# Gate and up products of a dense SwiGLU layer: high and low input joined into one 512-column matmul, and the bank's halves summed by VectorE

## The chip, the cores and the metric

The kernel runs on one core of one Trainium2 chip. The metric is the device time of one execution in microseconds (us); lower is better.

## What is computed

The reference is a two-layer decoder trunk over 256 tokens of width 1024. Each layer has a token mixer (a gated linear recurrence beside differential attention), a SwiGLU channel mixer, and a per-layer embedding. The channel mixer is dense in layer 0 and picks two of eight experts per token in layer 1. The change touches the dense one:

```python
D_MODEL, SEQ, D_FF = 1024, 256, 3584

def swiglu(h, w_gate, w_up, w_down):
    return (jax.nn.silu(h @ w_gate) * (h @ w_up)) @ w_down

h = rmsnorm(x, norm_g[i, 2])
if i % 2 == 0:
    f = swiglu(h, ffn_w_gate[i // 2], ffn_w_up[i // 2], ffn_w_down[i // 2])
```

## The kernel before

All products are in float32 of reduced precision (fp32r), made more exact by splitting both operands: a high part that TensorE takes as it is, and a low part that holds the rest. A product is the sum of three: high by high, high by low, low by high.

**Chunks.** Weights arrive from memory in chunks of 1 MB, each in one of six `raw` slots of 128 x 2048. ScalarE writes the high part of a chunk into one of three `whi` slots, in two halves (`hi`; in the dense stage L1005); VectorE then writes the low part into `wlo` (`lo`, L1208; in the dense stage L1612). TensorE waits for each half of the low part (`s_lo`), uses the chunk, and reports each half as used (`s_pe`), on which ScalarE waits before it writes the high part of the chunk three further on. SyncE issues the load of a chunk when the low part of the chunk six before it is done (L517).

**The dense stage.** The 3584 hidden channels are cut into 14 pairs of chunks: for pair `s` a gate chunk and an up chunk, each all of the 1024 input channels (8 tiles `k`) by 256 hidden channels (2 tiles `t`). The first two pairs are written out, the other twelve run in a loop of two turns of six. The weights are held in the array and the input moves: `HH` and `HL`, the high and low part of the normalised input, 128 x 8 x 256 each. `chunk8` goes through `k` and `t` and issues the three products of 256 columns by `three` (L1921):

```python
for t in range(2):
    ins = three(B[bank][:, SEQ * t:SEQ * t + SEQ], wslot(b), x,
                (A, slice(256 * k + P * t, 256 * k + P * t + P)), (A, k, A), True,
                k == 0 and t == 0, k == KT - 1)
```

So one PSUM bank of 512 columns holds a chunk's result, 256 tokens for each `t`. Gate chunks use banks 0 and 2 in turn and up chunks 1 and 3. The first chunk of all is `chunk8_first` (L1959, L1961, L1967), which takes the low input last.

**The eviction.** On VectorE `dense` makes, for each of the two chunks, the low part of the chunk three further on and then the chunk's result: `scaled` (L1292) multiplies the bank by `RINV`, the inverse norm of each token, into `FS` (gate) or `FA` (up). ScalarE applies Silu to `FS` (L1008); VectorE multiplies, `FA` = `FS` x `FA` (L1623); ScalarE writes the high part `FH` (L1010), and VectorE the low part `FL` (L1626). The semaphores are `f_g` (gate evicted), `f_u` (up evicted), `f_s` (Silu done), `f_a` (product done), `f_h` and `f_l`. TensorE waits for `f_g` of the pair two before it begins a gate chunk and for `f_a` of that pair before an up chunk.

**The down products.** Fourteen further chunks (`down`) hold the activations and move the weights, 512 columns a matmul (L1910). `three_turned` reads those 512 columns in interleaved halves. They add into banks 4 to 7 (`Z_BANK`).

All four engines run their own instruction lists in the order in which the code issues them; the order of the work is written out by hand.

Of the kernel before, what the change touches and what calls it, by code (L numbers as in the profile page):

```python
# [8 lines left out]
ALU = mybir.AluOpType  # L9
ACT = mybir.ActivationFunctionType  # L10
AX = mybir.AxisListType
F32 = mybir.dt.float32
F32R = mybir.dt.float32r
# [3 lines left out]
P = 128  # L17
# [48 lines left out]
def bass_hybrid_rglru_diffattn_moe(nc, x, p, positions, norm_g, w_in, conv_w, conv_b, lru_wa, lru_ba, lru_wx,  # L66
# [4 lines left out]
    with ctx:  # L71
# [4 lines left out]
        def at(name, off, shape, dt=F32):  # L76
            return nc.alloc_sbuf_tensor_at(name, shape, dt, offset=off)
# [47 lines left out]


        a0 = arena
        HH = at("HH", a0, [P, KT, SEQ], F32R)
        HL = at("HL", a0 + 8 * KB, [P, KT, SEQ], F32R)
        o_rin = a0 + 16 * KB  # L130
        a1 = beside(o_rin, HELD)
        RIN = at("RIN", o_rin, [P, KT, SEQ + 3])
# [119 lines left out]
        def sem(name):  # L252
            return ctx.enter_context(nc.semaphore(name))
# [80 lines left out]
        s_hl = sem("s_hl")  # L334
        f_g = sem("f_g")
        f_u = sem("f_u")
        f_s = sem("f_s")
        f_a = sem("f_a")
        f_h = sem("f_h")
# [99 lines left out]
        block = ctx.enter_context(nc.Block())  # L439

        Z_BANK = ((4, 5), (6, 7))
        M_BANK = ((6, 7), (3, 5))
        PP_BANK = ((0, 4), (1, 5))
        PP_LAST = (5, 0)
# [736 lines left out]
        def _(dve):  # L1181
# [16 lines left out]
            def bank2(n):  # L1198
                return B[n][:, :].rearrange("p (t s) -> p t s", t=2)
# [51 lines left out]
            def inverse_row(i, bank):  # L1251
                dve.wait_ge(s_rt, i)
                link(v.tensor_copy(RINV[:, :], B[bank][:, 0:SEQ]))
# [36 lines left out]
            def scaled(dst, src):  # L1290

                return v.tensor_tensor(dst, src, RINV[:, :].unsqueeze(1).to_broadcast([P, 2, SEQ]), ALU.mult)  # L1292
# [310 lines left out]
            def dense(s, b, it):  # L1603

                q = (b - FFN0) // 2 % 2
                fs, fa = (t[:, q, :].rearrange("p (t s) -> p t s", t=2) for t in (FS, FA))
                for n in range(2):
                    nb = b + n + SPL
                    for e in range(2):
                        dve.wait_ge(s_hi, 2 * nb + e + 1 + 24 * it)  # L1610
                        r = slice(HC * e, HC * e + HC)
                        v.tensor_tensor(wlo[nb % SPL][:, r], raw[nb % RAW][:, r], whi[nb % SPL][:, r].bitcast(F32),  # L1612
                                        ALU.subtract).then_inc(s_lo, 1)
                    if n == 0:
                        if isinstance(s, int) and s == 0:
                            inverse_row(2, 6)
                        scaled(fs, bank2(2 * q)).then_inc(f_g, 1)
                    else:
                        ins = scaled(fa, bank2(2 * q + 1))
                ins.then_inc(f_u, 1)  # L1620
                dve.wait_ge(f_u, s + 1)
                dve.wait_ge(f_s, s + 1)
                v.tensor_tensor(fa, fs, fa, ALU.mult).then_inc(f_a, 1)  # L1623
                dve.wait_ge(f_h, s + 1)
                to = bass.ds(2 * s, 2) if not isinstance(s, int) else slice(2 * s, 2 * s + 2)
                v.tensor_tensor(FL[:, to, :], fa, FH[:, to, :].bitcast(F32), ALU.subtract).then_inc(f_l, 1)  # L1626
# [271 lines left out]
        def _(pe):  # L1898
# [30 lines left out]
            def split(b, e, jobs=0, turns=0):  # L1929

                pe.wait_ge(s_lo, 2 * b + e + 1 + 2 * FFN * jobs + 24 * turns)
# [3 lines left out]
            def chunk8(b, x, bank, ready=None, jobs=0, turns=0):  # L1935

                for k in range(KT):
                    if k % 4 == 0:
                        split(b, k // 4, jobs, turns)
                    if ready:  # L1940
                        ready(k)
                    for t in range(2):
                        ins = three(B[bank][:, SEQ * t:SEQ * t + SEQ], wslot(b), x,
                                    (A, slice(256 * k + P * t, 256 * k + P * t + P)), (A, k, A), True,
                                    k == 0 and t == 0, k == KT - 1)
                    if k % 4 == 3:
                        ins.then_inc(s_pe, 1)

# [329 lines left out]

            def dense(s, b, it):

                q = (b - FFN0) // 2 % 2
                for n in range(2):
                    pe.wait_ge(f_a if n else f_g, s + 1)
                    first = isinstance(s, int) and s == 0 and n == 0
                    if first:
                        pe.wait_ge(s_pp, 1)
                        chunk8_first(b, 1, 0)
                    elif isinstance(s, int) and s == 0:
                        pe.wait_ge(s_pp, 2)
                        chunk8(b + n, (HH, HL), 1, scales)  # L2290
                    else:
                        chunk8(b + n, (HH, HL), 2 * q + n, None, 0, it)

            def scales(k):

# [15 lines left out]
                             (A, 2 * d + k, slice(P * blk, P * blk + P)), False, d == 0 and k == 0, d == 13 and k == 1)  # L2311

            pe.wait_ge(s_pp, 4)
            for d in range(12):
                pe.wait_ge(f_l, d + 1)
                for k in range(2):
                    for blk in range(BLK):
                        for h in range(2):
                            ins = down(d, k, blk, h)
                    ins.then_inc(s_pe, 1)  # L2320
# [177 lines left out]
```

## Time and profile before

| | before |
|---|---|
| median of 3 runs | 1761.08 us (1759.01 to 1761.35) |
| profiled execution | 1763.04 us, span 1761.4 us |
| TensorE busy | 1723.9 us (98%) |
| VectorE busy | 1475.7 us (84%) |
| ScalarE busy | 1288.7 us (73%) |
| mean granted clock of TensorE | 0.995 |

Times of instructions are from one execution, recorded by the profiler, on the core's own clock from the start of the span. PE is TensorE, PEld its weight loads, DVE VectorE, ACT ScalarE, SP SyncE. The ends of matmuls are modelled and overlap with the next: their starts tell how far apart they stand. The start of a VectorE or ScalarE operation can lie before the recorded end of the one in front of it, for the same reason.

### The profile page before, as it was taken

What the parts mean: (1) busy time and instruction counts of PE and PEld (TensorE: products, weight loads), DVE (VectorE), ACT (ScalarE), POOL (GpSimd) and SP (SyncE); (2) the same over time, 40 slices, a digit from 0 to 9 for tenths busy, and PEclk for the clock granted to TensorE, in tenths of its full rate; (3) what the DMA queues carried; (4) which work ended last, traced back from release to release, by engine and by line L of the source; (5) the groups of instructions that cost most, each with busy time, mean ns of one, the idle gap of its engine ahead of it and who ended that gap; (6) DMA issues with size and microseconds to landing.
All of it is one profiled execution on the core that took longest, in us unless ns stands there. A gap on an engine that the chain in (4) does not pass through costs nothing.

```text
span 1761.4 us, 28085 instructions
## 1 busy us (share of the span) xinstructions
PE 1723.9 (98%) x9691; PEld 1535.7 (87%) x9691; DVE 1475.7 (84%) x1930; ACT 1288.7 (73%) x1713; POOL 104.8 (6%) x137
## 2 busy tenths in 40 slices
PE   8999999999999999999999999999999999999997
PEld 8987889999889987887888888888888888888885
DVE  7887667666468887678998999999999999999996
ACT  6747647444467657557888888888888888888777
POOL 1210000000010300002001001010010100100200
PEclk9999999999999999999999999999999999999999
DMA  9764556655654754557999999999999999999992
GB/s 304 216 189 141 168 187 199 196 194 193 207 184 151 233 170 140 197 179 240 404 397 407 404 387 404 393 409 404 394 403 390 406 404 393 408 397 399 404 365 77
DMA packets 206412, 516.93 MB, mean 293 GB/s; under 512 B 10754, under 2 KB 73092, under 8 KB 206340
## 3 DMA queue, kind: packets, MB, share of 16 engines
q1 hardware_dynamic: 198768, 493.81, 76.3%
q0 software_dynamic: 7248, 22.06, 3.8%
q8 instruction: 43, 0.70, 0.2%
q14 instruction: 29, 0.24, 0.0%
q10 hardware_dynamic: 324, 0.12, 0.0%
HBM read 503.87 MB, written 7.88 MB: 291 GB/s over the span
## 4 chain that ended last, share of the span: by engine, by line
PE 80%; DVE 10%; ACT 6%; DMA 2%; issue 2%; DVEq 0%; SPq 0%; ACTq 0%
PE bank L1910 60%; PE bank L1921 14%; DVE wlo L1208 4%; ACT whi L698 1%; PE bank L2444 1%; DMA raw<-in_moe_w_gate_dram 1%; ACT SC L904 1%; PE bank L2066 1%; DMA raw<-in_moe_w_down_dram 1%; ACT SQJ L709 1%; DVE SC L1362 0%; DVE RIN L1334 0%; ACT SC L899 0%; DVE HL L1226 0%; DMA raw<-in_ple_w_gate_dram 0%
## 5 line engine op out<-in xcount | busy, mean ns | idle before, releaser
L1208 DVE TENSOR_TENSOR wlo<-raw,whi 128x1024 fp32r<-128x1024 f32 x880 | 1027.5, 1221 | 148.3 <-ACT whi L698 147.6
L698 ACT ACTIVATE whi<-raw 128x1024 fp32r<-128x1024 f32 x880 | 913.9, 1055 | 260.8 <-PE bank L1910 203.4
L1910 PE MATMUL bank<-whi,XGH 128*128 128x512 f32 x896 | 343.9, 384 | 4.3 <-DVE wlo L1208 3.6
L1910 PE MATMUL bank<-wlo,XGH 128*128 128x512 f32 x896 | 340.3, 380 | 0.0
L1910 PE MATMUL bank<-whi,XGL 128*128 128x512 f32 x896 | 340.3, 380 | 0.0
L1921 PE MATMUL bank<-HH,whi 128*128 128x256 f32 x912 | 255.0, 280 | 0.0
L1921 PE MATMUL bank<-HL,whi 128*128 128x256 f32 x912 | 252.6, 277 | 0.0
L1921 PE MATMUL bank<-HH,wlo 128*128 128x256 f32 x912 | 252.6, 277 | 0.0
L1910 PEld LDWEIGHTS bank<-whi,XGH 128*128 128x128 f32 x896 | 169.8, 190 | 29.0 <-DVE wlo L1208 5.0
L1910 PEld LDWEIGHTS bank<-whi,XGL 128*128 128x128 f32 x896 | 169.8, 189 | 24.2
L1910 PEld LDWEIGHTS bank<-wlo,XGH 128*128 128x128 f32 x896 | 169.8, 189 | 23.1
L1910 PE MATMUL bank<-whi,ATH 128*128 128x512 f32 x448 | 172.5, 385 | 0.0
L1921 PEld LDWEIGHTS bank<-HH,whi 128*128 128x128 f32 x912 | 171.3, 188 | 0.8 <-issue 0.7
L1921 PEld LDWEIGHTS bank<-HH,wlo 128*128 128x128 f32 x912 | 171.6, 188 | 0.0
L1921 PEld LDWEIGHTS bank<-HL,whi 128*128 128x128 f32 x912 | 171.5, 188 | 0.2
L1910 PE MATMUL bank<-wlo,ATH 128*128 128x512 f32 x448 | 169.8, 379 | 0.0
L1910 PE MATMUL bank<-whi,ATL 128*128 128x512 f32 x448 | 169.8, 379 | 0.0
L1910 PE MATMUL bank<-whi,HH 128*128 128x512 f32 x272 | 105.6, 388 | 0.0
L1910 PE MATMUL bank<-wlo,HH 128*128 128x512 f32 x272 | 103.8, 382 | 0.0
L1910 PE MATMUL bank<-whi,HL 128*128 128x512 f32 x272 | 103.7, 381 | 0.0
L1910 PEld LDWEIGHTS bank<-whi,ATL 128*128 128x128 f32 x448 | 84.7, 189 | 12.0
L1910 PEld LDWEIGHTS bank<-wlo,ATH 128*128 128x128 f32 x448 | 84.8, 189 | 11.2
(361 smaller groups left out, 2170.1 us busy)
## 6 DMA issues: line engine op xcount, KB each, us to landing
raw<-in_moe_w_gate_dram SPq DMA_DIRECT2D x112, 1024.0 KB, 8.0
raw<-in_moe_w_up_dram SPq DMA_DIRECT2D x112, 1024.0 KB, 8.6
raw<-in_moe_w_down_dram SPq DMA_DIRECT2D x112, 1024.0 KB, 7.5
raw<-in_w_in_dram SPq DMA_DIRECT2D x56, 1024.0 KB, 6.1
raw<-in_ffn_w_gate_dram SPq DMA_DIRECT2D x14, 1024.0 KB, 5.0
raw<-in_ffn_w_up_dram SPq DMA_DIRECT2D x14, 1024.0 KB, 5.0
raw<-in_ffn_w_down_dram SPq DMA_DIRECT2D x14, 1024.0 KB, 4.9
raw<-in_w_proj_a_dram SPq DMA_DIRECT2D x8, 1024.0 KB, 5.0
```

Of the source, the lines that this page charges most:

```text
L698: nc.scalar.activation(whi[b % SPL][:, r], raw[b % RAW][:, r], ACT.Copy).then_inc(s_hi, 1)
L709: nc.scalar.activation(SQJ[:, 0:src.shape[-1]], src, ACT.Square, accum_out=sums).then_inc(s, 1)
L904: ins = nc.scalar.activation(r, r, ACT.Exp, bias=AMX[:, q, 2 + m:3 + m], scale=HD ** -0.5, accum_out=ASUM[:, q, 2 + m:3 + m])
L1208: v.tensor_tensor(wlo[b % SPL][:, r], raw[b % RAW][:, r], whi[b % SPL][:, r].bitcast(F32), ALU.subtract).then_inc(s_lo, 1)
L1910: ins = mm(dst, a, turns(b), start=start and n == 0, stop=stop and n == 2, skip_group_check=True)
L1921: ins = mm(dst, a, b, start=start and n == 0, stop=stop and n == 2, skip_group_check=True)
L2066: ins = mm(bank[:, SEQ * kind:SEQ * kind + SEQ], BD[:, kind, t, :], U[:, t, :], start=True, stop=True)
L2444: ins = nc.tensor.transpose(B[6][:, P * i:P * i + P], MA[:, f % 2, P * i:P * i + P], IDENT[:, :])
```

## The change

`HH` and `HL` become the two halves of one tile `HHL` at the same addresses. In the twelve pairs of the loop a new function `chunk8_joined` takes the place of `chunk8`. For each `k` and `t` it issues two matmuls in place of three: the high weights are held once while 512 columns move, the 256 of the high input and then the 256 of the low input, into the two halves of one bank; then the low weights are held while the high input moves, into the first half. Each chunk now needs two banks, one for each `t`, which are taken from a ring of three pairs, (0, 1), (6, 7) and (2, 3). TensorE waits for the bank's release three chunks back (`f_u` or `f_g`), not two pairs back.

VectorE sums the halves of each of the two banks with a `tensor_reduce` of 256 x 2 elements into `FS` or `FA`, waits for both (new semaphore `f_r`), and then multiplies by `RINV` in place.

The first two pairs keep the three matmuls of 256 columns, in banks 0, 1, 2 and 4 (`FIRST_FFN`), with waits for `s_pp`. Ahead of the down products TensorE also waits for `f_u` of the pair before last.

```diff
-        HH = at("HH", a0, [P, KT, SEQ], F32R)
-        HL = at("HL", a0 + 8 * KB, [P, KT, SEQ], F32R)
+        HHL = at("HHL", a0, [P, 2, KT, SEQ], F32R)
+        HH, HL = HHL[:, 0], HHL[:, 1]
...
+        FIRST_FFN = ((0, 1), (2, 4))
+        RING_FFN = ((0, 1), (6, 7), (2, 3))
...
+                    if isinstance(s, int):
+                        if (s, n) == (0, 0):
+                            inverse_row(2, 6)
+                        ins = scaled(fa if n else fs, bank2(FIRST_FFN[s][n]))
+                    else:
+                        for t, bank in enumerate(RING_FFN[(b - FFN0 + n) % 3]):
+                            ins = v.tensor_reduce((FA if n else FS)[:, q, SEQ * t:SEQ * t + SEQ],
+                                                  B[bank][:, :].rearrange("p (a n) -> p n a", a=2), AX.X, ALU.add)
+                        ins.then_inc(f_r, 1)
+                        dve.wait_ge(f_r, 2 * s + n - 3)
+                        ins = scaled(fa if n else fs, fa if n else fs)
                     if n == 0:
-                        if isinstance(s, int) and s == 0:
-                            inverse_row(2, 6)
-                        scaled(fs, bank2(2 * q)).then_inc(f_g, 1)
-                    else:
-                        ins = scaled(fa, bank2(2 * q + 1))
+                        ins.then_inc(f_g, 1)
                 ins.then_inc(f_u, 1)
...
+            def chunk8_joined(b, banks, turns):
+
+                for k in range(KT):
+                    if k % 4 == 0:
+                        split(b, k // 4, 0, turns)
+                    for t in range(2):
+                        cols = slice(256 * k + P * t, 256 * k + P * t + P)
+                        mm(B[banks[t]][:, :].rearrange("p (a n) -> p a n", a=2), whi[b % SPL][:, cols],
+                           HHL[:, :, k, :], start=k == 0, stop=False, skip_group_check=True)
+                        ins = mm(B[banks[t]][:, 0:SEQ], wlo[b % SPL][:, cols], HH[:, k, :], start=False,
+                                 stop=k == KT - 1, skip_group_check=True)
+                    if k % 4 == 3:
+                        ins.then_inc(s_pe, 1)
...
             def dense(s, b, it):
 
-                q = (b - FFN0) // 2 % 2
                 for n in range(2):
-                    pe.wait_ge(f_a if n else f_g, s + 1)
-                    first = isinstance(s, int) and s == 0 and n == 0
-                    if first:
-                        pe.wait_ge(s_pp, 1)
-                        chunk8_first(b, 1, 0)
-                    elif isinstance(s, int) and s == 0:
-                        pe.wait_ge(s_pp, 2)
-                        chunk8(b + n, (HH, HL), 1, scales)
+                    if isinstance(s, int):
+                        pe.wait_ge(s_pp, 2 * s + n + 1 if s == 0 else 3)
+                        if (s, n) == (0, 0):
+                            chunk8_first(b, 1, 0)
+                        else:
+                            chunk8(b + n, (HH, HL), FIRST_FFN[s][n], scales if s == 0 else None)
                     else:
-                        chunk8(b + n, (HH, HL), 2 * q + n, None, 0, it)
+                        if n:
+                            pe.wait_ge(f_g, s + 2)
+                        else:
+                            pe.wait_ge(f_u, s - 1)
+                        chunk8_joined(b + n, RING_FFN[(b - FFN0 + n) % 3], it)
...
             pe.wait_ge(s_pp, 4)
+            pe.wait_ge(f_u, FT // 2 - 1)
```

How this stands in the instruction order. On TensorE, the first gate chunk of the loop, before; the name behind the arrow is the moving tile, then the held one, with the column count:

```order
L1931 ISA [waits f_g]
L1921 MATMUL bank<-HH,whi_55 128x256 [waits s_lo]
L1921 MATMUL bank<-HL,whi_55 128x256
L1921 MATMUL bank<-HH,wlo_58 128x256
L1921 MATMUL bank<-HH,whi_55 128x256
L1921 MATMUL bank<-HL,whi_55 128x256
```

And the same place with the change, with bank numbers:

```order
L1941 ISA [waits f_u]
L1966 MATMUL bank6<-HHL_89,whi0_55 128x512 [waits s_lo]
L1968 MATMUL bank6<-HHL_89,wlo0_58 128x256
L1966 MATMUL bank7<-HHL_89,whi0_55 128x512
L1968 MATMUL bank7<-HHL_89,wlo0_58 128x256
L1966 MATMUL bank6<-HHL_89,whi0_55 128x512
```

Each group of three narrow matmuls is now a wide one and a narrow one; the wait at the chunk's start names the up eviction instead of the gate's.

On VectorE, the first pair of the loop, before:

```order
L1612 TENSOR_TENSOR wlo_58<-raw_49,whi_55 128x1024 [waits s_hi]
L1292 TENSOR_TENSOR FS<-bank,RINV 128x512
L1610 REGISTER_ALU
L1612 TENSOR_TENSOR wlo_59<-raw_50,whi_56 128x1024 [waits s_hi]
L1610 REGISTER_ALU
L1612 TENSOR_TENSOR wlo_59<-raw_50,whi_56 128x1024 [waits s_hi]
L1292 TENSOR_TENSOR FA<-bank,RINV 128x512
L1621 ISA
L1623 TENSOR_TENSOR FA<-FS,FA 128x512 [waits f_s,f_u]
L1626 ISA [waits f_h]
L1626 TENSOR_TENSOR FL<-FA,FH 128x512
```

And with the change:

```order
L1615 TENSOR_TENSOR wlo_58<-raw_49,whi_55 128x1024 [waits s_hi]
L1623 TENSOR_REDUCE FS<-bank 128x256 x2
L1626 ISA
L1295 TENSOR_TENSOR FS<-FS,RINV 128x512 [waits f_r]
...
L1623 TENSOR_REDUCE FA<-bank 128x256 x2
L1626 REGISTER_ALU
L1295 TENSOR_TENSOR FA<-FA,RINV 128x512 [waits f_r]
L1631 REGISTER_ALU
L1633 TENSOR_TENSOR FA<-FS,FA 128x512 [waits f_s,f_u]
L1636 ISA [waits f_h]
L1636 TENSOR_TENSOR FL<-FA,FH 128x512
```

The two reduces and a wait stand ahead of each multiply by `RINV`, which now reads and writes SBUF; everything else keeps its place.

## Rows read from the trace of the kernel before

**Rows 1.** The page's head and its first part: busy us (share of span) x instructions.
```profile
span 1761.4 us, 28085 instructions
...
PE 1723.9 (98%) x9691; PEld 1535.7 (87%) x9691; DVE 1475.7 (84%) x1930; ACT 1288.7 (73%) x1713; POOL 104.8 (6%) x137
```

**Rows 2.** The page's chain that ended last: shares by engine, then by line.
```profile
PE 80%; DVE 10%; ACT 6%; DMA 2%; issue 2%; DVEq 0%; SPq 0%; ACTq 0%
PE bank L1910 60%; PE bank L1921 14%; DVE wlo L1208 4%; ACT whi L698 1%; PE bank L2444 1%; DMA raw<-in_moe_w_gate_dram 1%; ACT SC L904 1%; PE bank L2066 1%; DMA raw<-in_moe_w_down_dram 1%; ACT SQJ L709 1%; DVE SC L1362 0%; DVE RIN L1334 0%; ACT SC L899 0%; DVE HL L1226 0%; DMA raw<-in_ple_w_gate_dram 0%
```

**Rows 3.** The chain in order of time: start us, us, what.
```profile
288.88 144.18 PE bank L1921 x1272
433.06 69.94 PE bank L1910 x324
```

**Rows 4.** Stretches of the loop's twelve pairs and of the down products.
```profile
core 0: us, PE busy (x) PEld busy (x) DVE busy (x) ACT busy (x) POOL busy (x), PEclk, DMA share, GB/s
302.54:433.06 130.52, 130.52 (x1153) 130.52 (x1152) 89.22 (x97) 63.67 (x74) 0.00 (x0) 1.00 0.60 198
433.06:503.00 69.94, 69.94 (x326) 61.13 (x326) 35.09 (x34) 30.51 (x34) 0.54 (x1) 1.00 0.62 210
```

**Rows 5.** VectorE in order of time, one pair: start us, us, what [idle before].
```profile
340.58 2.36 DVE L1612 TENSOR_TENSOR wlo<-raw,whi 128x1024 fp32r<-128x1024 f32 x2
342.86 0.68 DVE L1292 TENSOR_TENSOR FS<-bank,RINV 128x512 f32<-128x512 f32 x1
344.43 1.23 DVE L1612 TENSOR_TENSOR wlo<-raw,whi 128x1024 fp32r<-128x1024 f32 x1 [0.89 <-ACT whi L1005]
347.15 1.23 DVE L1612 TENSOR_TENSOR wlo<-raw,whi 128x1024 fp32r<-128x1024 f32 x1 [1.50 <-ACT whi L1005]
348.30 0.68 DVE L1292 TENSOR_TENSOR FA<-bank,RINV 128x512 f32<-128x512 f32 x1
349.01 0.69 DVE L1623 TENSOR_TENSOR FA<-FS,FA 128x512 f32<-128x512 f32 x1
350.64 0.69 DVE L1626 TENSOR_TENSOR FL<-FA,FH 128x512 f32 x1 [0.94 <-ACT FH L1010]
351.46 2.36 DVE L1612 TENSOR_TENSOR wlo<-raw,whi 128x1024 fp32r<-128x1024 f32 x2
```

**Rows 6.** ScalarE in order of time, the up chunk of that pair.
```profile
343.34 1.06 ACT L1005 ACTIVATE whi<-raw 128x1024 fp32r<-128x1024 f32 x1 [1.66 <-PE bank L1921]
346.06 1.06 ACT L1005 ACTIVATE whi<-raw 128x1024 fp32r<-128x1024 f32 x1 [1.66 <-PE bank L1921]
```

**Rows 7.** Groups of VectorE instructions by form: count | busy us, mean ns | idle before.
```profile
L1612 DVE TENSOR_TENSOR wlo<-raw,whi 128x1024 fp32r<-128x1024 f32 x56 | 67.3, 1223 | 31.2 <-ACT whi L1005 29.9
...
L1623 DVE TENSOR_TENSOR FA<-FS,FA 128x512 f32<-128x512 f32 x14 | 9.7, 692 | 0.5
...
L1253 DVE COPY RINV<-bank 128x256 f32<-128x256 f32 x3 | 1.3, 418 | 0.0
...
L1577 DVE TENSOR_REDUCE SM<-TT 128x4 f32<-128x256 f32 x1 | 0.4, 420 | 0.0
```

**Rows 8.** VectorE in order of time, the first gate chunk.
```profile
292.94 0.69 DVE L1292 TENSOR_TENSOR FS<-bank,RINV 128x512 f32<-128x512 f32 x1
293.54 1.22 DVE L1612 TENSOR_TENSOR wlo<-raw,whi 128x1024 fp32r<-128x1024 f32 x1
```

**Rows 9.** TensorE in order of time, narrow matmuls behind wide ones.
```profile
523.70 0.38 PE L1910 MATMUL bank<-whi,HL 128*128 128x512 f32 x1
523.92 0.28 PE L1921 MATMUL bank<-whi,HH 128*128 128x256 f32 x1
...
524.62 0.28 PE L1921 MATMUL bank<-whi,HH 128*128 128x256 f32 x1
```

**Rows 10.** The chain in order of time, transposes of 128 columns in layer 1.
```profile
839.57 0.44 PE bank L2444 x4
```

More of the change, by code:

```diff
@@ L336, in bass_hybrid_rglru_diffattn_moe @@
         f_u = sem("f_u")
+        f_r = sem("f_r")
         f_s = sem("f_s")
```

## The prediction

> **What bounds the kernel now.** I began with the page's first part: TensorE is busy for 98% of the span, VectorE for 84% [rows 1]. Busy shares of pipelined matmuls say little, so next came the chain of waits: 80% of it is TensorE, 14% the line of the 256-column products (L1921), and DMA ends only 2% [rows 2]. In order of time the chain shows the stretch that matters: from 288.88 to 433.06 us it is one unbroken piece of 1272 matmuls of L1921, which is half a chunk and 26 more of the 28 gate and up chunks, and the down products follow with 324 matmuls in 69.94 us [rows 3]. Nothing interrupts TensorE there: its time is a count of matmuls by their spacing, and whatever a chunk takes less moves all that follows forward. The rest of the chain is the same engine's work [rows 2].
>
> The spacings come from the table by stretches [rows 4]. The 24 chunks that the loop runs are 1152 matmuls of 256 columns in 130.52 us, 113.3 ns each (the 0.28 us that a row gives as a matmul's duration [rows 9] overlap). The down matmuls, 512 columns each, stand 69.94/324 = 215.9 ns apart. The clock is 1.00 of 2.4 GHz in both. At that clock 256 columns take 106.7 ns and 512 take 213.3, so a matmul costs 6.6 ns above its columns when narrow and 2.5 ns when wide. VectorE is busy for 89 us of those 130, ScalarE for 64 [rows 4].
>
> **What the change removes on TensorE.** Per k and output tile t, three matmuls of 256 columns become one of 512 and one of 256: the columns stay 768, one matmul and one weight load go. In the 24 loop chunks that is 24 x 8 x 2 = 384 groups; the first four chunks keep the old form. The new spacing of the 256 one is taken as 113.3. That of the 512 one is not in the trace: every 512-column matmul of this kind reads its moving tile in interleaved halves, and this one reads 256 columns of HH and then 256 of HL, 8 KB apart. Its bounds are 215.9 (the down matmuls [rows 4]) and 2 x 113.3 = 226.6 (nothing gained by joining). I take 215.9: the bytes and addresses are those of before, the extra 6.6 ns goes with a weight load at every 256 columns, and here a load has 512 columns to hide behind. Saved per group: 339.9 - 215.9 - 113.3 = 10.7 ns; by 384 it is **4.1 us**, bounds 0 and 4.1.
>
> The 256 one could be cheaper too, since the load ahead of it now hides under the wide one. Its lower bound is the four transposes of 128 columns in 0.44 us [rows 10], 110 ns with a load each, which would give 3.3 x 384 = 1.3 us more; its upper one is the 117 ns of the 256-column matmuls from 523.92 to 524.62 us (six gaps), where activations are held, weights move and wide matmuls have gone before [rows 9], which costs 1.4 us. I keep 113.3, the row of the same operands.
>
> The Trainium skill ("TensorE: Matmul & The Clock Gate", section "Wait — 56ns, not 53.3ns?") puts the spacing at columns over the clock plus about 2.5 ns, whatever the width: the wide rows agree, the narrow ones (113.3 against 109.2) do not. By the page, before and after differ by one such 2.5 ns, 1.0 us in all; by the rows 4.1. The rows decide.
>
> **What it adds on VectorE.** The gate or up bank was read once by a multiply (L1292). Now each of two banks goes through a reduce of 512 elements to 256, and the multiply follows on SBUF behind a wait for both (f_r). What an operation takes from VectorE is the distance to the next start: a multiply of 512 elements out of PSUM holds it 0.60 us when the next one doesn't wait [rows 8], 0.71 when the next waits for its result (348.30 to 349.01 [rows 5]). The trace has one reduce, 256 elements to 4, 420 ns, beside a copy of 256 at 418 [rows 7]: an element read costs the same in both. I take 0.60 for a reduce, 0.71 for the second of a chunk. The multiply keeps its time (SBUF to SBUF 692 ns [rows 7], 0.68 before [rows 5]). So a chunk gains 0.60 + 0.71 = 1.31 us of VectorE, a pair 2.62.
>
> A pair's work today, from the starts [rows 5]: 2.28 for two low splits, 0.60 (gate sum), 2.28, 0.71 (up sum), 1.63 from the product to FL (ScalarE's FH between), 0.82 to the next split: 8.32 of 10.88 us. With 2.62 more it is **10.94 us, against 32 x (0.2159 + 0.1133) = 10.53 us that TensorE will want**. VectorE becomes the slower of the two by 0.41 us a pair, and the question is whether twelve pairs are enough for that to show.
>
> They are just too few. Today VectorE waits for ScalarE twice a pair, 0.89 and 1.50 us [rows 5], and ScalarE for TensorE; a bank's sum ends 2.9 us behind the chunk (346.06, when ScalarE sees the chunk's end [rows 6], to 348.30 + 0.68 [rows 5]). Adding the operations one by one with the spacings above, the gate sums end 4.4 us behind in the first joined pair, 5.7 in the second, then 0.41 more each, 9.4 us in the last but one. TensorE wants a pair of banks back after two further chunks, 10.53 us: 1.0 us to spare at the end. The low splits that TensorE waits for keep 3 us or more, and in the down products, where a chunk takes 24 x 215.9 ns = 5.2 us of TensorE and 2.3 of VectorE, the debt is gone before FL of the last pair is wanted (twelve chunks later). Each 0.01 us on the reduce's 0.60 adds 0.04 a pair: free up to 0.62, beyond it about 0.4 us in all for each.
>
> **Free edits.** HHL is HH and HL in the same place. The waits for s_pp in the second pair are for copies that ScalarE issues before the splits the same chunks need anyway. The wait for f_u before the down products is met in the pair before last. ScalarE has no operation more; its FH comes later with VectorE's product, and the next high split behind it: the 0.82 above holds that. SP issues a load when a low split six chunks ahead of the one it feeds is done, so up to 6.5 us of lag leave over 20 of its 32 us; DMA share is 0.60 [rows 4]. If that cover were gone TensorE would wait for each late load in full.
>
> **Sum.** 4.1 us off, nothing on the other side. The profiled execution took 1763.04 us (span 1761.4); less 4.1 it is 1758.9. The median of the runs, 1761.08, is 2 us lower, and my number is put against it: **1757.0 us**. A measurement of this kernel tells about 0.2%, 3.5 us, from no change, so the forecast lies barely beyond it.
>
> **Rivals.**
> - *The joined matmul costs its 6.6 ns or more.* If the excess belongs to a weight load or to this reading order, it spaces at 219.9 (saving 6.7 x 384 = 2.6 us, 1758.5) up to 226.6 (1761.1). For it: no wide matmul here reads straight. Against: the same bytes.
> - *The narrow one gets cheaper as well.* 110 ns as [rows 10]: 5.4 us saved, 1755.7. VectorE is then at its limit, 10.43 against 10.94 a pair.
> - *VectorE sets the pace, and the kernel is slower.* The place is TensorE's wait for f_g or f_u at a chunk's start, the bank not yet summed; it decides from 0.62 us per reduce. At 0.70 the saving is 0.9 us (1760.2), at 0.72 nil. A reduce that also pays for each result, 256 x 1.04 ns (1.223 less 0.692 us over 512 elements [rows 7]) = 0.27 us, would hold VectorE 0.87: 25 x 0.4 less 4.1 is 5.9 us slower, 1767.0. For it: the margin is 1.0 us after twelve pairs. Against: the reduce in the trace costs what a copy costs, though with 4 results only.
> - *The change doesn't do what it says*: waits on loop counters or the new ring serialise chunks from the start. The instruction order shows the three bank pairs in turn and one wait per chunk, so little speaks for it.
>
> The Trainium skill ("VectorE: DVE Perf Modes", section "Rules for kernel authors") warns against this very step: "Expect 1× — it's the slowest DVE op. Consider restructuring". One element per cycle is also what the fp32 multiplies here run at, so by rule and row alike a reduce is 0.60 and the sum stands; what speaks against the change is the count of such operations, not their rate.
>
> **How the numbers follow.** Forecast 0.45; joined matmul dearer 0.20; narrow one cheaper 0.10; VectorE's pace with a time not slower than before by 0.2% 0.12, slower 0.10; not as described 0.03. The range takes the cheaper narrow matmul with a microsecond of scatter (1754.5) and goes up to a reduce of 0.76 (1762.5). Faster by over 0.2%: three quarters of the forecast's 0.45, all of the 0.10, a little of the others, 0.49. Slower: 0.11. Within 0.2%: 0.40.
>
> **What the profile after should show.** Between 302.5 us and the first down matmul: 768 matmuls of the new lines in 126.4 us (32 a pair, 10.53), with no wait of TensorE for VectorE; reduces of about 0.68 us starting 0.60 apart; VectorE without waits for the high split in the later pairs; the down products beginning near 428.9. The prediction is wrong if TensorE waits at chunk starts, if a group of two takes over 331 ns, if a reduce lasts over 0.71 us, or if a gain at 428.9 is not at the end.

## The result, and the profile after

| | before | after |
|---|---|---|
| median, runs side by side | 1760.66 us (1759.01 to 1762.01) | 1766.39 us (1764.45 to 1768.63) |
| ratio, 95% interval | | 1.0033 (1.0024 to 1.0043) |
| profiled execution, span | 1763.04 us, 1761.4 us | 1766.39 us, 1764.8 us |
| first down matmul | 433.06 us | 438.15 us |
| first expert matmul of layer 1 | 809.5 us | 814.7 us |
| mean granted clock | 0.995 | 0.997 |

The kernel is 5.7 us slower, where 4.1 us less had been forecast. The page's head, its busy times and the shares of its chain by engine, after:

```profile
span 1764.8 us, 27395 instructions
...
PE 1724.8 (98%) x9307; PEld 1519.5 (86%) x9307; DVE 1504.9 (85%) x1978; ACT 1287.2 (73%) x1713; POOL 105.4 (6%) x137
...
PE 82%; DVE 9%; ACT 6%; issue 2%; DMA 0%; DVEq 0%; ACTq 0%; SPq 0%
```

TensorE has 384 matmuls and 384 weight loads fewer than in [rows 1] and is busy for 0.9 us longer. The chain of waits in order of time (start us, us, what) shows the same place as [rows 3]; it now follows the wide and narrow matmuls one by one, so that only their neighbours stand as long pieces:

```profile
288.87 13.62 PE bank L1931 x120
...
438.15 69.94 PE bank L1920 x324
```

The joined matmuls lie between 288.87 + 13.62 = 302.49 and 438.15: 135.66 us for 384 groups of one wide and one narrow, **353.3 ns a group**, where before it was 339.9 for three narrow ones and the forecast said 329.2. By this measure, which the stretches below use, they take 5.1 us more than before, and the down products behind them take their 69.94 us as ever. The table by stretches, as [rows 4]:

```profile
core 0: us, PE busy (x) PEld busy (x) DVE busy (x) ACT busy (x) POOL busy (x), PEclk, DMA share, GB/s
302.20:438.15 135.95, 135.95 (x772) 118.16 (x771) 117.27 (x143) 62.42 (x74) 0.00 (x0) 1.00 0.56 187
438.15:508.00 69.85, 69.85 (x326) 61.04 (x325) 37.06 (x37) 30.50 (x34) 0.54 (x1) 1.00 0.63 216
```

TensorE is busy without a gap at full clock: no wait appears in the stretch. So the matmuls themselves stand further apart. TensorE in order of time (start us, us, what):

```profile
341.88 0.40 PE L1966 MATMUL bank<-HHL,whi 128*128 128x512 f32 x1
342.12 0.28 PE L1968 MATMUL bank<-HHL,wlo 128*128 128x256 f32 x1
342.24 0.40 PE L1966 MATMUL bank<-HHL,whi 128*128 128x512 f32 x1
...
345.77 0.40 PE L1966 MATMUL bank<-HHL,whi 128*128 128x512 f32 x1
```

From 341.88 to 345.77 are eleven groups, 353.6 ns each. The rows are rounded to 10 ns; over all starts of the loop in the trace, a wide matmul holds TensorE for 235.0 ns (bare columns: 213.3) and a narrow one for 118.3. Of the loss against the forecast, 19.1 ns a group are the wide one's and 5.0 the narrow one's. The recorded durations say it too: the down and expert matmuls of the same width last 379 ns, as they did before, and these 397 in the median (least, median, most; first and last start):

```profile
L1966 PE MATMUL bank<-HHL,whi x384: 388/397/398, 302.3 to 437.6; 128*128 128x512 f32 x192
L1968 PE MATMUL bank<-HHL,wlo x384: 281/281/282, 302.5 to 437.9; 128*128 128x256 f32 x192
...
L1920 PE MATMUL bank<-whi,XGH x896: 378/379/634, 814.7 to 1685.5; 128*128 128x512 f32 x180
```

VectorE in order of time, most of a pair, to be laid beside [rows 5]:

```profile
343.16 2.36 DVE L1615 TENSOR_TENSOR wlo<-raw,whi 128x1024 fp32r<-128x1024 f32 x2
345.44 1.28 DVE L1623 TENSOR_REDUCE FS<-bank 128x256 f32<-128x512 f32 x2
346.75 0.69 DVE L1295 TENSOR_TENSOR FS<-FS,RINV 128x512 f32<-128x512 f32 x1
347.36 1.22 DVE L1615 TENSOR_TENSOR wlo<-raw,whi 128x1024 fp32r<-128x1024 f32 x1
348.83 1.22 DVE L1615 TENSOR_TENSOR wlo<-raw,whi 128x1024 fp32r<-128x1024 f32 x1 [0.25 <-ACT whi L1008]
...
354.46 2.36 DVE L1615 TENSOR_TENSOR wlo<-raw,whi 128x1024 fp32r<-128x1024 f32 x2
```

The two reduces take 346.75 - 345.44 = 1.31 us, just what was forecast for them. A pair comes back after 354.46 - 343.16 = 11.30 us, which is TensorE's 32 x 353.3 ns. The second half of the up chunk's low split starts 1.47 us behind the first; two that nothing holds start 2.36 - 1.22 = 1.14 apart. So 0.33 us of the pair is waiting for the high split, and VectorE's own work is 10.97 us: here it was never put to its limit. A gate sum ends 5.6 us behind its chunk in every pair from the second on, 5.7 us before TensorE wants the banks again.

### The profile page after: what moved, and what is told of

It reads as the page before. It is cut to its first block, busy times and chain, and to the rows that moved or that the text cites. A ratio compares the mean times of both kernels' runs of the same rounds, so it can differ in the third digit from the quotient of the medians.

```text
span 1764.8 us, 27395 instructions
## 1 busy us (share of the span) xinstructions
PE 1724.8 (98%) x9307; PEld 1519.5 (86%) x9307; DVE 1504.9 (85%) x1978; ACT 1287.2 (73%) x1713; POOL 105.4 (6%) x137
## 4 chain that ended last, share of the span: by engine, by line
PE 82%; DVE 9%; ACT 6%; issue 2%; DMA 0%; DVEq 0%; ACTq 0%; SPq 0%
PE bank L1920 63%; PE bank L1931 6%; PE bank L1966 5%; DVE wlo L1211 4%; PE bank L1968 3%; ACT whi L701 1%; PE bank L2470 1%; ACT SC L907 1%; PE bank L2090 1%; ACT SQJ L712 1%; DVE SC L1365 1%; DVE RIN L1337 0%; ACT SC L902 0%; DVE U L1311 0%; DVE HHL L1229 0%
## 5 line engine op out<-in xcount | busy, mean ns | idle before, releaser
L1931 PE MATMUL bank<-HHL,whi 128*128 128x256 f32 x1056 | 185.4, 280 | 0.0
L1920 PE MATMUL bank<-whi,HHL 128*128 128x512 f32 x544 | 167.9, 382 | 0.0
L1931 PEld LDWEIGHTS bank<-HHL,whi 128*128 128x128 f32 x1056 | 160.4, 188 | 1.0 <-issue 0.7
L1931 PE MATMUL bank<-HHL,wlo 128*128 128x256 f32 x528 | 146.6, 278 | 0.0
L1966 PE MATMUL bank<-HHL,whi 128*128 128x512 f32 x384 | 135.7, 397 | 0.0
L1920 PEld LDWEIGHTS bank<-whi,HHL 128*128 128x128 f32 x544 | 102.9, 189 | 14.9 <-issue 0.7
L1968 PE MATMUL bank<-HHL,wlo 128*128 128x256 f32 x384 | 107.9, 281 | 0.0
L1920 PE MATMUL bank<-wlo,HHL 128*128 128x512 f32 x272 | 103.1, 379 | 0.0
L1931 PEld LDWEIGHTS bank<-HHL,wlo 128*128 128x128 f32 x528 | 99.7, 189 | 0.0
```

The lines of the kernel that those rows point to most:

```text
L1920: ins = mm(dst, a, turns(b), start=start and n == 0, stop=stop and n == 2, skip_group_check=True)
L1931: ins = mm(dst, a, b, start=start and n == 0, stop=stop and n == 2, skip_group_check=True)
L1966: mm(B[banks[t]][:, :].rearrange("p (a n) -> p a n", a=2), whi[b % SPL][:, cols], HHL[:, :, k, :], start=k == 0, stop=False, skip_group_ch ...
L1968: ins = mm(B[banks[t]][:, 0:SEQ], wlo[b % SPL][:, cols], HH[:, k, :], start=False, stop=k == KT - 1, skip_group_check=True)
```

## The experiments

Three theories stood after the result. A: the joined matmul, which reads 256 columns of HH and then 256 of HL, costs its own extra time. B: something else in the new arrangement (two banks in turn, the ring, the reduces on PSUM beside TensorE's writes) slows TensorE. C: a wide matmul that alternates with a narrow one pays for the alternation. (The text quoted next gives the letter C to another: VectorE's longer work holds TensorE up. The profile above speaks against that one, since TensorE waits nowhere in the stretch.)

### The joining alone undone

```diff
-mm(B[banks[t]][:, :].rearrange("p (a n) -> p a n", a=2), whi..., HHL[:, :, k, :], ...)
+for a in range(2):
+    mm(B[banks[t]][:, SEQ * a:SEQ * a + SEQ], whi..., HHL[:, a, k, :], start=k == 0 and a == 0, ...)
```

> The changed kernel, but each wide matmul of the loop is issued as two of 256 columns (high input into the bank's first half, low input into its second), so banks, ring, reduces and waits stay and only the joining is undone. Theory A (the wide matmul, by its straight reading order, runs slower than its columns): three narrow ones at 113.3 ns again, 339.9 ns a group, the loop's stretch 130.5 us, the time within 1 us of before (about 1761). Theory B (the cost comes from the two banks that TensorE writes in turn, whatever the width): a group stays at 354 ns, the time at 1766. Theory C (VectorE's longer work holds TensorE up): as B, with waits of TensorE at chunk starts.

This is e1: 1761.49 us (1758.70 to 1763.42), ratio to before 1.0007 (0.9998 to 1.0017). The chain in order of time:

```profile
288.61 13.62 PE bank L1931 x120
...
432.79 69.94 PE bank L1920 x324
```

432.79 - 302.23 = 130.56 us, 340.0 ns a group: before's figure. The banks, the ring, the waits, the reduces and the second wait on VectorE are all still there and cost nothing. The whole loss comes with the one matmul that was two: its own time, and that of the narrow one behind it. B falls.

### The same 512 columns, high and low in turn

The tile is the same; only the order in which TensorE walks through it changes: column n of HH, column n of HL (8 KB away), column n + 1 of HH. The bank is then written straight, so high and low results alternate in it, while the low weights' product and VectorE's reduce are left as they were: what they add up is no longer the three products of one token. Every instruction and size stays.

```diff
-mm(B[banks[t]][:, :].rearrange("p (a n) -> p a n", a=2), ..., HHL[:, :, k, :], ...)
+mm(B[banks[t]][:, :], ..., HHL[:, :, k, :].rearrange("p a n -> p n a"), ...)
```

> The changed kernel with the wide matmul reading high and low input column by column in turn (interleaved, as the down products read their weights) in place of 256 and then 256; the narrow one still writes the bank's first 256 columns, so the sums mix tokens: the computation of the gate and up products is changed, the amount of work is not. Theory A (reading order): the wide one falls from 235 to 216 ns, a group to 329 to 334, the loop's stretch to 126.5 to 128.3 us. Theory B (two banks in turn): 354 ns a group, unchanged. A third theory (the 8 KB between the two halves costs a jump): interleaving jumps at every column, so it would get slower, over 235 ns.

This is e2: 1758.85 us, one run, beside 1760.77 before.

```profile
288.93 13.62 PE bank L1931 x120
...
430.55 69.94 PE bank L1920 x324
```

128.00 us, 333.3 ns a group, 20 less than with the straight order. The wide ones now last 378 ns each and hold TensorE for 215.0 ns, the narrow ones, unchanged and straight, still for 118.3. So the distance of 8 KB between the halves is no price; a joined matmul can be as cheap as a down matmul. What makes the wide one dear is the straight walk; the narrow one pays its 5 ns behind a wide one of either walk.

### Wide ones together, narrow ones together

Half a chunk's eight wide matmuls first, then its eight narrow ones.

```diff
+for wide in (True, False):
+    for k in range(4 * e, 4 * e + 4):
+        for t in range(2):
```

> The changed kernel with each half chunk's eight wide matmuls issued first and its eight narrow ones after them, still in two banks in turn. Theory A: wide ones among themselves at 235 ns, narrow ones among themselves at 113.3 as before the change. Theory B (banks in turn): both as in the changed kernel, 235 and 118. If a wide one is only slow because a narrow one stands before it: 216 and 113, a group at 329.

This is e4: 1765.27 us, one run, between 1760.77 before and the 1766.39 of the change. The chain in order of time within the loop:

```profile
381.22 1.86 PE bank L1968 x8
383.08 0.91 PE bank L1971 x8
```

1.86/8 = 232.5 ns for a wide one, 0.91/8 = 113.8 for a narrow one. The wide one is nearly as dear among its own kind: alternation accounts for 2.5 of its 235 ns, and C is not its main trouble. It is that of the narrow one: the seven of eight that follow a narrow one are back at before's 113.3, the one that follows a wide one stands at 118.3. Together a wide and a narrow one take 346 ns here, against 353.3 in turn and 339.9 before: so about half of the loss, 7.0 of 13.4 ns, goes with the alternation, most of it the narrow one's. C falls for one half and stands for the other.

### Two pieces of HH in place of HH and HL

```diff
+kk = min(k, KT - 2)
-HHL[:, :, k, :]
+HH[:, kk:kk + 2, :]
```

Left out here: the high by low product, since the wide matmul reads 512 adjacent columns of the high input instead.

> The changed kernel with the wide matmul reading 512 adjacent columns (two neighbouring k of the high input) in place of 256 of the high and 256 of the low input 8 KB further: the gate and up products are changed, the amount of work is not. If the jump of 8 KB inside a matmul is what costs: wide at 226 ns or less, a group at 340 to 345. If the straight order itself costs, jump or none: 235 and a group at 354, as in the changed kernel.

This is e7: 1765.61 us, one run. The first down matmul starts at 437.85, behind the row `x120` from 288.57: 135.66 us, 353.3 ns a group, the change's own figure to the tenth. Whether the second 256 columns lie next door or 8 KB off is all the same.

### The address of the moving tiles

A constant places the arena of moving operands 192 bytes into a raster of 256; here it goes to 0, for the whole kernel.

```diff
-MOVING, HELD = 192, 0
+MOVING, HELD = 0, 0
```

> The changed kernel with the arena of the activations moved by 64 bytes of the 256 by which SBUF addresses are laid out against the weight slots (MOVING 192 to 0). If the cost of straight reads comes from where the moving and the held tile lie against each other: wide and narrow of the joined chunks change by over 3 ns, either way, and the narrow ones of the mixers with them. If it lies in the order of a read alone: 235 and 118 stay within 1 ns.

This is e8: 1770.79 us, one run.

```profile
292.07 14.39 PE bank L1931 x120
...
442.14 69.94 PE bank L1920 x324
```

The narrow straight matmuls ahead of the loop go from 13.62/120 = 113.5 to 14.39/120 = **119.9 ns**: their spacing hangs on where the tile lies; whether its own place counts or that against the weights, which stayed, the run doesn't tell. The joined groups keep their mean, 442.14 - 306.46 = 135.68 us, 353.3 ns, but not their parts: in the trace the wide ones now vary from 232 to 241 ns and the narrow ones from 113 to 120, repeating every three groups, where in the change nearly all stand at 235 and 118. So 113.3 was never a constant of width, but one of width, order, place and neighbour.

### Joined, with the token halves in turn

If the straight walk is the price, the tokens can be walked otherwise: column n, then column n + 128, 512 bytes on, and so to the end, for both the wide and the narrow matmul. The bank then holds the tokens in that order, and VectorE's reduce puts them back as it reads.

```diff
-v.tensor_reduce((FA if n else FS)[...], B[bank][:, :].rearrange("p (a n) -> p n a", a=2), ...)
+v.tensor_reduce((FA if n else FS)[...].rearrange("p (h n) -> p h n", h=2),
+                B[bank][:, :].rearrange("p (a n h) -> p h n a", a=2, h=2), ...)
-mm(..., HHL[:, :, k, :], ...)
+mm(B[banks[t]][:, :], ..., HHL[:, :, k, :].rearrange("p a (h n) -> p a n h", h=2), ...)
-mm(..., HH[:, k, :], ...)
+mm(..., HH[:, k, :].rearrange("p (h n) -> p n h", h=2), ...)
```

> The changed kernel, computing the same, with every moving tile of the joined chunks read in interleaved token halves (token n, then token n + 128, of the high input and then of the low), and VectorE's reduce putting the tokens back in order by its access pattern. Theory A: wide 216 ns, narrow 109 to 113, a group 325 to 329, the loop's stretch 124.8 to 126.4 us and 4 to 6 us off the time before: 1755 to 1757, unless VectorE's pace then shows. Theory B: no change from 354 ns.

This is e5: 1755.20 us (1753.94 to 1756.37), ratio to before **0.9969 (0.9957 to 0.9980)**. The chain, and TensorE in order of time:

```profile
288.64 13.62 PE bank L1932 x120
...
379.71 0.38 PE L1967 MATMUL bank<-HHL,whi 128*128 128x512 f32 x1
379.93 0.27 PE L1970 MATMUL bank<-HHL,wlo 128*128 128x256 f32 x1
380.04 0.38 PE L1967 MATMUL bank<-HHL,whi 128*128 128x512 f32 x1
```

The down products begin at 428.28: 126.02 us, 328.2 ns a group, a nanosecond under the forecast's 329.2. By the starts in the trace the wide one takes 218.4 and the narrow one 109.1, 327.5 together; the rest is one wait, shown below. With TensorE as fast as forecast, VectorE's part of the forecast is tested for the first time. Two starts of the low split in later pairs:

```profile
407.38 2.36 DVE L1615 TENSOR_TENSOR wlo<-raw,whi 128x1024 fp32r<-128x1024 f32 x2
409.66 1.28 DVE L1623 TENSOR_REDUCE FS<-bank 128x256 f32<-128x512 f32 x2
...
418.36 2.36 DVE L1615 TENSOR_TENSOR wlo<-raw,whi 128x1024 fp32r<-128x1024 f32 x2
```

A pair takes VectorE 10.98 us here against TensorE's 32 x 327.5 ns = 10.48 us, so it falls behind by 0.5 us a pair. The gate sums end 4.6 us behind their chunk in the first joined pair, 6.0 in the second and 10.5 in the last but one, where the forecast had 9.4. At that point the ring is used up. TensorE around the start of the last up chunk and, below the dots, VectorE's multiply of the gate:

```profile
422.51 0.27 PE L1970 MATMUL bank<-HHL,wlo 128*128 128x256 f32 x1
422.77 0.48 PE L1967 MATMUL bank<-HHL,whi 128*128 128x512 f32 x1
423.09 0.27 PE L1970 MATMUL bank<-HHL,wlo 128*128 128x256 f32 x1
...
421.95 0.69 DVE L1295 TENSOR_TENSOR FS<-FS,RINV 128x512 f32<-128x512 f32 x1
```

The first wide matmul of the chunk starts 0.26 us behind the narrow one, not 0.11, right after the gate's multiply ends at 422.64, and the next start comes 0.32 us later, not 0.22. The semaphore for which an up chunk waits at its start is `f_g`, so this is TensorE waiting for VectorE, once: with the 0.1 us by which the next start comes later it costs 0.26 us in all; the list of waits leaves it out, since the recorded end of the matmul in front covers it. The eleven pairs before cost nothing, but of the 1.0 us that the forecast had to spare nothing was left.

### The same, with one reduce more

Into a scratch tile that nobody reads, ahead of each chunk's two reduces.

```diff
+v.tensor_reduce(SQJ[:, 0:SEQ], B[RING_FFN[(b - FFN0 + n) % 3][0]][:, :].rearrange("p (a n) -> p n a", a=2), ...)
```

> The interleaved joined kernel with one reduce more per chunk on VectorE, of the first bank into scratch, so 0.60 us more per chunk and 1.20 per pair: a pair's work on VectorE is 12.1 us against TensorE's 10.5. By the pace arithmetic of the prediction the lag then eats the ring's slack after four or five pairs, TensorE waits at chunk starts for f_g and f_u, and the kernel takes about 11 us more than the interleaved joined one, 1766. If the ring hides more than that arithmetic says, or VectorE overlaps operations further: under 5 us more.

This is e9: 1766.98 us, one run, 11.8 more than without. TensorE's waits between 300 and 446 us (us in total, times, longest):

```profile
PE bank L1969 <- DVE FS L1295: 10.0, 7, 1.5
```

Now TensorE waits at chunk starts for the gate eviction, and the down products begin at 440.21, 11.9 us later. This is the rival in which VectorE sets the pace, made to happen: it is real. The change, with its slow matmuls, was 5.7 us away from it; at the forecast's pace of TensorE, in e5, its first wait is already there.

### Only the order, in the kernel before

Two runs: e6 keeps the three narrow matmuls per group, walks the token halves in turn in the 24 loop chunks, and evicts with one multiply for each `t`; e13 does so with one multiply of 512. In both the second of the written-out pairs is walked so too, but its results are not put back in order; that pair's gate and up values stand at wrong tokens, whatever the quoted text says of the same result.

```diff
-xh, xl = HH[:, k, :], HL[:, k, :]
+xh, xl = turns(HH[:, k, :]), turns(HL[:, k, :])
-scaled(fs, bank2(2 * q))
+v.tensor_tensor(dst.rearrange("p t (h n) -> p t h n", h=2),
+                bank[:, :].rearrange("p (t n h) -> p t h n", t=2, h=2), ..., ALU.mult)
```

> The kernel before (three narrow matmuls a group, one bank, no reduce), with the moving tiles of the loop's twelve pairs read in interleaved token halves and the multiply by RINV, one for each t, putting the tokens back. It computes the same. Theory A, narrow form (a straight read of 256 columns costs 113.3 ns, an interleaved one 109 to 110): a group of three at 328 to 330 ns, the loop's stretch 126 to 127 us, 3.5 to 4.5 us off the time before, so that nearly all of the 5.6 us gained by the interleaved joined kernel is the reading order's and joining itself gives 1 us or less. If the order only matters for wide matmuls: 113.3 ns stays, and the time of before.

> The kernel before with interleaved token halves in the loop's twelve pairs alone, three narrow matmuls a group, and each eviction one multiply of the whole bank that puts the tokens back. It computes the same. If the order is worth the same here as in the kernel with all its products interleaved: 111.7 ns a matmul, the loop's stretch 128.6 us against 130.5, about 1.9 us off before, 1758.5 to 1759 and within what a measurement tells from no change. What the joined kernel with the same order gained beyond it (5.6 less 1.9) is then the joining's, about 3.5 us. If joining gives nothing of its own: 1755 to 1756 here too.

e6 took 1758.59 us, ratio 0.9984 (0.9975 to 0.9994); e13 took 1759.79, ratio 0.9997 (0.9987 to 1.0006). Their chains agree; this is e13's:

```profile
291.62 139.36 PE bank L1965 x1248
430.98 69.95 PE bank L1916 x324
```

139.36/1248 = **111.7 ns**, against 144.18/1272 = 113.3 [rows 3]. On 1152 loop matmuls that is 1.9 us, and the first down and expert matmuls start 2.1 and 2.0 us earlier than before. That is less than these medians can tell: one of the two twins lies outside the noise, the other within, and I count the traces' 2 us. Per group the order alone gives 335.0, not the 328 to 330 that e6's text expected; with joining it is 328.2. So joining, once it is walked well, is worth 6.8 x 384 = 2.6 us by itself (7.5 ns a group without e5's one wait), not the 4.1 of the forecast nor the 3.5 of e13's text. The narrow matmul reaches 109 only behind a wide one.

### The order everywhere, without and with joining

The same walk for all products whose input moves in 256 columns: the written-out pairs, and the mixers' chunks in both layers.

```diff
+def across(x, k):
+    return x[:, k, :].rearrange("p (h n) -> p n h", h=2)
+def scaled_turned(dst, bank):
+    return v.tensor_tensor(dst.rearrange("p t (h n) -> p t h n", h=2), B[bank]... "p (t n h) -> p t h n" ..., ALU.mult)
```

> The kernel before with interleaved token halves in every product that holds weights and moves HH and HL (the dense stage and chunks 0 to 11 and 16 to 19 of both mixers), the evictions putting the tokens back through their access patterns. It computes the same. Theory A: 2880 narrow matmuls at 109 to 110 in place of 113.3 ns, 10 us less work for TensorE; where VectorE or ScalarE bounds the mixers, less of it shows: 5 to 10 us off the time before, 1751 to 1756. If four-dimensional access patterns slow the evictions, their rows get longer than 684 ns.

> The joined kernel with interleaved token halves in the loop, and the same interleaving in every other product that holds weights and moves HH and HL. It computes the same. If the two gains are each TensorE's own: 328.6 ns a group in the loop (as in the interleaved joined kernel) and 111.7 in place of 113.3 ns on the other 1728 narrow matmuls, 2.8 us beyond 1755.2: about 1752.5, 8 us or 0.5% off before. If the mixers' pace is VectorE's or ScalarE's instead: 1755, nothing beyond the interleaved joined kernel.

Without joining, e10: 1755.93 us (1754.69 to 1760.26), ratio 0.9980 (0.9970 to 0.9990). With joining, e11: **1752.40 us (1751.21 to 1757.53), ratio 0.9960 (0.9948 to 0.9972)**, the lowest median of all. That it lies 0.1 us from what was expected is in part luck: its seven runs spread over 6 us, and the profiled one took 1755.79. The chain without joining, then the same line's neighbours with it:

```profile
287.95 142.04 PE bank L1959 x1272
429.99 69.95 PE bank L1919 x324
```

```profile
287.66 13.40 PE bank L1970 x120
427.08 69.95 PE bank L1930 x324
```

142.04/1272 and 13.40/120 are 111.7 ns again, where e10's text had expected 109 to 110. The eviction that puts the tokens back costs VectorE nothing:

```profile
L1298 DVE TENSOR_TENSOR FS<-bank,RINV 128x512 f32<-128x512 f32 x14 | 9.6, 684 | 0.0
```

684 ns, where the straight one has 0.68 us [rows 5].

### Quarters in turn

The joined kernel with the token quarters in turn, 256 bytes from one column to the next, in place of halves.

```diff
-"p a (h n) -> p a n h", h=2
+"p a (h n) -> p a n h", h=4
```

> The interleaved joined kernel with token quarters (four rows of 64 tokens read in turn) in place of halves. If what matters is only that neighbouring columns are not read from neighbouring addresses: wide 218 and narrow 110 ns as with halves, a group at 328.6. If the distance between columns read in turn matters: a group moves by over 2 ns, either way.

This is e12: 1792.33 us, one run, 32 us slower than before.

```profile
288.50 13.62 PE bank L1932 x120
...
379.59 0.45 PE L1967 MATMUL bank<-HHL,whi 128*128 128x512 f32 x1
379.88 0.31 PE L1970 MATMUL bank<-HHL,wlo 128*128 128x256 f32 x1
380.02 0.45 PE L1967 MATMUL bank<-HHL,whi 128*128 128x512 f32 x1
...
465.95 69.94 PE bank L1921 x324
```

163.83 us, 426.6 ns a group, 283.3 and 143.3, at clock 1.00: 0.55 to 0.56 ns a column for both widths, where a column takes 0.417 by the clock. A walk can cost a third more, and turning the columns is no remedy in itself; the distance decides.

## Why the prediction was wrong

**What bounds the kernel: right.** The stretch is TensorE's alone, a count of matmuls by their spacing, and its change is found again in all that follows: 5.1 us at the first down matmul, 5.2 at the first expert matmul, 5.7 in the medians.

**The step that failed** is the spacing of the joined matmul, "I take 215.9", and more than the choice its bounds: "2 x 113.3 = 226.6 (nothing gained by joining)" was put down as the upper one. The measured value is 235. Two narrow matmuls are the sum that joining undoes, but no ceiling for what it makes; a matmul that reads in an order the trace doesn't show has no upper bound from those that read in another. The reason given, "the bytes and addresses are those of before", leaves out the order in which they come, which the same paragraph had named as what sets this matmul apart from every wide one in the trace. The 6.6 ns above the columns were then given to the weight load. The runs show that place and walk move them: at an unchanged count of loads they go from 6.8 to 13.2 with the tile's address (e8) and to 5.0 with the token halves in turn (e10). A part for the load is not ruled out: in the walk of halves the 5.0 of a narrow matmul among its own kind fall to 2.4 behind a wide one (e5), where the load ahead of it could hide under more columns.

**The narrow one** was taken at 113.3, bounds 110 and 117. It stands at 118.3, again outside. The rows that gave the 117 [rows 9] were read as narrow matmuls behind wide ones, but only the first of them stands directly behind one; they show another tile, not this neighbour. Of the neighbour the trace had no row for the operands in question.

The two together are 19.1 + 5.0 = 24.1 ns (353.3 - 329.2), by 384 it is 9.3 us: the whole way from 4.1 us gained to 5.1 us lost.

**The Trainium skill's rule.** "TensorE: Matmul & The Clock Gate", section "Wait — 56ns, not 53.3ns?", has the spacing as columns over the clock and some 2.5 ns, from a run in bf16. The down matmuls (215.9), e2's wide ones (215.0) and e5's narrow ones (109.1) agree with it; the straight ones disagree, at 235 against 215.8 and at 113.3 to 119.9 against 109.2, and so do the halves in turn, by less, at 218.4 and 111.7. By it the change would have gained 1 us. Neither the rule nor my rows held, and for the same cause: neither asks how the moving tile is walked or what stands in front.

**The rivals.** "The joined matmul costs its 6.6 ns or more" had the right place and the right suspicion ("no wide matmul here reads straight"), but its price ended at no gain. The narrow one did not get cheaper behind a straight wide one; in e5's walk it did, to 109. "VectorE sets the pace" did not come about: TensorE waits for no bank in the change or in e1, and once, for 0.26 us, in e5. "The change doesn't do what it says" fell as well. So the slower side got its 0.11 from a mechanism that was sound and idle, and nothing from the one that decided.

**VectorE: its terms right, the slack too large.** A reduce holds it 0.60 us and the second of a chunk 0.71: measured 1.31 for both. A pair's work was forecast at 10.94 and is 10.97. That twelve pairs hide it was right in the change by luck, since TensorE was 0.8 us a pair slower than forecast. At the forecast's pace (e5) VectorE loses 0.49 us a pair, not 0.41, and starts 0.2 to 0.3 further back; the spare 1.0 us is gone in the last but one pair, and TensorE waits, if only for 0.26 us. With one reduce more it waits for 10 (e9). The Trainium skill ("VectorE: DVE Perf Modes", section "Rules for kernel authors") calls the reduce the slowest operation; the trace doesn't bear that out for these: a reduce of 512 elements is recorded with 681 ns and a multiply of as many with 684.

**The free edits: right.** HHL's place, the new waits and the ring cost nothing together (e1, 340.0 against 339.9 ns). Of the signs named, the one that a group over 331 ns would prove the forecast wrong is the one that spoke; the waits of VectorE for the high split grew short (0.25 us) rather than vanished, since TensorE was slower than thought.

**Left open.** Why a straight walk of 512 columns costs more than two of 256, why a straight narrow matmul behind a wide one costs 5 ns more, what share the weight load has, and what makes a distance of 256 bytes so dear. The experiments show that the walk does it, not how. Other places of the tile than two, and other distances than those shown, were not tried.

## What to carry to other kernels

Price a matmul that moves fp32r data by a row with the same width, the same walk through the moving tile and the same neighbours, and where no such row exists leave the upper bound open instead of closing it with the sum of what it replaces. Where the input moves straight, walking two far halves in turn and putting the order back in the eviction can be free time: here some 7 us of 1760 with the joining (0.9960, 0.9948 to 0.9972). Test the distance first: with 256 bytes in place of 512 the kernel was 32 us slower than before. Engine-pace arithmetic from start-to-start distances held to 0.03 us in 11 for one pair; over eleven pairs its errors added up to 1.1 us, as much as the slack that was to be judged.

## What the chip showed that was not expected

All at a granted clock of 1.00, operands fp32r, ns from one matmul to the next, from counts over a stretch, or, where two kinds alternate, as the mean over their starts in the trace:

| walk through the moving tile | 512 columns | 256 columns |
|---|---|---|
| straight, 4 bytes on | 235.0 (232.5 among its own kind) | 113.3 (119.9 with the arena at 0 in place of 192; 118.3 behind a wide one) |
| quarters in turn, 256 bytes | 283.3 | 143.3 |
| token halves in turn, 512 bytes | 218.4 | 111.7 (109.1 behind a wide one) |
| down products, as before | 215.9 | |
| high and low in turn, 8 KB | 215.0 | |

The straight wide matmul is dearer than two straight narrow ones together, by 8 ns (6 among its own kind), and in the walk of halves it is cheaper than two, by 5. VectorE, by contrast, reads every other column of PSUM at the price of a straight read: the multiply that puts the tokens back is recorded with 684 ns either way.
